# Convolution taps moved to later steps, and one subtraction put earlier, in a two-layer decoder step

## The reference, cut to what matters

```
h = rmsnorm(x);  z = h @ w_in          # one projection for all branches
y_a = mLSTM(q, k, v, gates)            # 4 heads of 128, decayed scores, matrix memory
u = glu_a * sigmoid(glu_b)
y_b = silu(layernorm(dwconv31(u)))     # depthwise, causal, 31 taps, 512 channels
y_c = sliding-window attention with sinks  # 8 query heads, 2 key heads, window 128
x += (g_a*y_a + g_b*y_b + g_c*y_c) @ w_out
x += (silu(dwconv3(h2 @ w_gate)) * (h2 @ w_up)) @ w_down
```

## Time and profile before

| | before |
|---|---|
| median of 3 runs | 1087.49 us |
| the profiled execution | 1089.15 us, span 1087.1 us |
| PE busy | 1028.8 us (95% of the span) |
| DVE busy | 782.5 us (72%) |
| ACT busy | 558.9 us (51%) |
| POOL busy | 38.3 us (4%) |
| mean granted clock of TensorE | 0.976 of full |

### The profile page before, as it was taken

One profiled execution on the slowest core, in us unless ns is written; L12 is line 12 of the kernel. 1 busy time (PEld: TensorE's weight loads), 2 busy tenths in 40 slices (PEclk: granted clock), 3 DMA queues, 4 the chain that ended last, 5 costly groups with the idle time before them and its releaser, 6 DMA issues.

```text
span 1087.1 us, 19523 instructions
## 1 busy us (share of the span) xinstructions
PE 1028.8 (95%) x7898; PEld 976.9 (90%) x7898; DVE 782.5 (72%) x1489; ACT 558.9 (51%) x1040; POOL 38.3 (4%) x55
## 2 busy tenths in 40 slices
PE   5999999899898999999979999998998989999997
PEld 3998889788898999999979998897888989999996
DVE  4577896656787778775565879874769877877563
ACT  3545555645534656553344456644654546665432
POOL 0010000003000000000000200000120000000000
PEclk9999999899999999999989999998999999999999
DMA  9654536355445676556576645462654657665561
GB/s 251 148 139 122 137 98 157 97 143 144 151 136 155 193 217 174 169 158 177 146 182 156 159 106 153 112 177 81 156 166 144 168 138 238 184 177 170 166 185 48
DMA packets 318643, 167.92 MB, mean 154 GB/s; under 512 B 25270, under 2 KB 317478, under 8 KB 318490
## 3 DMA queue, kind: packets, MB, share of 16 engines
q1 hardware_dynamic: 318410, 165.87, 56.0%
q10 hardware_dynamic: 144, 0.80, 0.2%
HBM read 160.11 MB, written 9.71 MB: 156 GB/s over the span
## 4 chain that ended last, share of the span: by engine, by line
PE 77%; DVE 9%; ACT 6%; DMA 4%; issue 3%; SPq 0%; DVEq 0%; ACTq 0%
PE ps_tile L883 16%; PE ps_tile L884 15%; PE ps_tile L885 15%; PE work L883 7%; PE work L885 7%; PE work L884 7%; ACT w_hi L1279 2%; DVE w_lo L1748 2%; DMA w_raw<-in_w_in 2%; DVE uc L1849 1%; DMA w_raw<-in_w_conv_out 1%; PE work L1117 1%; ACT scores L1413 1%; PE work L1119 1%; PE work L1127 1%
## 5 line engine op out<-in xcount | busy, mean ns | idle before, releaser
L1748 DVE TENSOR_TENSOR w_lo<-w_raw,w_hi 128x1024 fp32r<-128x1024 f32 (+1 forms) x288 | 341.4, 1192 | 135.0 <-ACT w_hi L1279 134.6
L1279 ACT ACTIVATE w_hi<-w_raw 128x1024 fp32r<-128x1024 f32 (+1 forms) x288 | 295.0, 1028 | 180.7 <-DMA w_raw<-in_w_in 78.3
L883 PE MATMUL ps_tile<-h_hi,w_hi 128*128 128x280 f32 (+2 forms) x944 | 284.7, 302 | 10.2 <-DVE h_lo L1758 10.2
L884 PE MATMUL ps_tile<-h_lo,w_hi 128*128 128x280 f32 (+2 forms) x944 | 277.0, 293 | 0.0
L885 PE MATMUL ps_tile<-h_hi,w_lo 128*128 128x280 f32 (+2 forms) x944 | 276.5, 293 | 0.0
L883 PEld LDWEIGHTS ps_tile<-h_hi,w_hi 128*128 128x128 f32 (+1 forms) x944 | 179.6, 190 | 16.9 <-issue 14.6
L884 PEld LDWEIGHTS ps_tile<-h_lo,w_hi 128*128 128x128 f32 (+1 forms) x944 | 179.4, 190 | 1.0
L885 PEld LDWEIGHTS ps_tile<-h_hi,w_lo 128*128 128x128 f32 (+1 forms) x944 | 179.0, 190 | 0.6
L883 PE MATMUL ps_tile<-xg_hi,w_hi 128*128 128x280 f32 (+1 forms) x368 | 107.7, 293 | 6.2 <-DVE x L1806 6.2
L1849 DVE SCALAR_TENSOR_TENSOR uc<-u_pad,vec,uc 128x272 f32<-128x272 f32 x240 | 108.4, 506 | 0.1
L885 PE MATMUL ps_tile<-xg_hi,w_lo 128*128 128x280 f32 (+1 forms) x368 | 107.2, 291 | 0.0
(11 more groups left out here) (348 smaller groups left out, 1836.7 us busy)
## 6 DMA issues: line engine op xcount, KB each, us to landing
w_raw<-in_w_in SPq DMA_DIRECT2D x98, 512.0 KB, 4.1
w_raw<-in_w_ffn_gate SPq DMA_DIRECT2D x44, 512.0 KB, 3.9
w_raw<-in_w_ffn_up SPq DMA_DIRECT2D x44, 512.0 KB, 3.9
w_raw<-in_w_ffn_down SPq DMA_DIRECT2D x32, 512.0 KB, 3.6
w_raw<-in_w_out SPq DMA_DIRECT2D x16, 512.0 KB, 3.6
w_raw<-in_w_ffn_down SPq DMA_DIRECT2D x14, 384.0 KB, 3.1
w_raw<-in_w_in SPq DMA_DIRECT2D x20, 256.0 KB, 3.6
c_head<-in_state_mlstm_c SPq DMA_DIRECT2D x8, 512.0 KB, 4.1
```

Source lines behind the costliest of these rows:

```text
L883: mm(out, hi[:, k, :], a_hi[:, k0 + k, f:T], start=first, stop=False, skip_group_check=True)
L884: mm(out, hi[:, k, :], a_lo[:, k0 + k, f:T], start=False, stop=False, skip_group_check=True)
L1279: go(h, r, ACT.Copy).then_inc(w_hi_ready, 1)
L1748: tt(lo, r, h.bitcast(F32), ALU.subtract).then_inc(w_split[n % SLOTS], 1)
```

## The change

`BUSY` gives other counts. In the attention steps 21 to 36 an odd step has 1 tap for 2, an even one 2 for 4. Steps 37, 38 and 42 have 5 for 4. Steps 43 to 50 have 7 for 4; these add up to more than 124, so that step 50 is left with 4. In a layer 24 taps leave steps 21 to 36, 3 go to steps 37 to 42 and 21 to steps 43 to 49.

On VectorE, `block_att_lo` moves ahead of `softmax_unit_2` within a step. Steps in which both stand are 29 (block 0, unit 3) and 33 (block 1, unit 5).

```diff
-BUSY = {10: 2, 14: 0, 15: 0, 16: 3, 17: 1, 18: 1, 19: 0, 20: 1, 39: 0, 40: 3, 41: 1, **{n: 2 for n in range(21, 37, 2)}}
+BUSY = {10: 2, 14: 0, 15: 0, 16: 3, 17: 1, 18: 1, 19: 0, 20: 1, 39: 0, 40: 3, 41: 1, 37: 5, 38: 5, 42: 5,
+        **{n: 1 if n % 2 else 2 for n in range(21, 37)}, **{n: 7 for n in range(43, 51)}}
 TAPS_AT = [BUSY.get(n, 4) if CONV_FROM <= n < CONV_TO else 0 for n in range(N_PIECES)]
...
                     if n == 20:
                         output_sample()
+                    if n - 1 in VALUES_AT[1::2]:
+                        block_att_lo(VALUES_AT.index(n - 1) // 2)
                     if n - 2 in SCORES_AT:
                         softmax_unit_2(SCORES_AT.index(n - 2))
                     if n == 22:
                         sample_att_lo()
-                    if n - 1 in VALUES_AT[1::2]:
-                        block_att_lo(VALUES_AT.index(n - 1) // 2)
```

## The result

The changed kernel takes 1093.14 us (median, 12 runs), the one before 1087.13, timed beside it: a ratio of 1.0056 (95% interval 1.0041 to 1.0071), or 6.0 us more (4.5 to 7.7). One of the twelve runs took 4555.12 us and is left out of the ratio; without it the median is 1092.92. A second measurement of the same pair (e8) gave 1.0058 (1.0039 to 1.0077). The forecast was +4.0 and 1091.5.

A forecast was written before the change was run, and what follows sets the result against it. TensorE was taken to set the pace, VectorE time counting only ahead of decay_d or att_lo products. Terms -3.3 + 1.9 + 0.5 + 4.9 gave +4.0 us, a median of 1091.5, range 1084 to 1097.

The forecast's parts named there:

- the second rival: VectorE bounds the attention steps, so both waits there go and mLSTM steps hide the taps: 1082, chance 0.08.
- the third: Rival: only step 43's taps cost, as TensorE comes later to step 48 anyway: -0.8, 1086.7, chance 0.17.
- a wait of about 2.4 in step 48: Sign that the forecast is right: TensorE waits about 2.4 us for decay_d in step 48 of both layers.
- The order, -3.3: Step 29's att_lo ahead of the softmax scaling shortens step 30: 2.2 us in layer 0, 1.06 in layer 1.
- The 1.2 for the low clock in layer 0: Part of the order's gain: step 30's 16 products take 1.86 us instead of 3.08 at full clock.
- Taps leaving the attention, 0: Steps 21 to 36 lose 24 taps a layer, 10 us of VectorE, with no gain in time.
- Step 43, +1.9: Three more taps ahead of head 0's decay_d: +1.24 us a layer, less 0.6 in all for low clock.
- Step 45, +0.5: Seven taps collide with GpSimd's gating product and end later: +0.25 us a layer, between 0 and 0.5.
- Steps 46 and 47, +4.9: Both tap blocks delay decay_d of head 2: +2.4 us in layer 0, +2.5 in layer 1.
- Steps 48 to 50, 0: decay_d of head 3 is 2.5 us later, but TensorE comes 2.4 later too: 0, at most 1.24.
- The first rival: The new wait in step 48 draws a low-clock stretch: +6.4 to +10 us, 1094 to 1097.5, chance 0.23.
- The sum: All terms for the whole kernel together: -3.3 + 1.9 + 0.5 + 4.9 = +4.0 us, median 1091.5.

The follow-up runs named there:

- e8: The changed kernel again, without edit, timed against the kernel before for a second profile: 1093.36 us, ratio 1.0058.
- e7: The control: the kernel before, without edit, timed against itself: 1087.01 us, ratio 0.9990.
- e3: The kernel before with 7 taps in step 43 for 4, leaving step 50 with 1: 1088.88 us, ratio 1.0010.
- e2: The kernel before with only the tap counts changed, the order as before: 1094.48 us, ratio 1.0065 to the kernel before.
- e5: The changed kernel with 4 taps in steps 43, 45, 46, 47, and 10 in 42, 12 in 44, 9 in 48, 8 in 49: 1095.77 us.
- e12: The changed kernel with step 43 empty and 11 taps in step 42: 1081.98 us, ratio 0.9966 to the kernel before.
- e6: The kernel before with the new order and step 43's four taps moved to step 42: 1076.65 us, ratio 0.9881.

## Why the prediction was right, and where it was not

- **The direction and the reason held.** The taps are free where they were, as the windows show, and are paid where they went. The two main paying places are those named, steps 44 and 48. With that the second rival is out (the attention steps did not get shorter by the taps that left), and so is the third (step 48 does wait). Of the signs named, one did not come: a wait of about 2.4 in step 48; it is 1.19 and 1.54.
- **The order, -3.3.** Measured alone -2.8 (-4.6 to -1.0). At equal clock it is 1.12 and 0.94, against the forecast's 1.0 and 1.06. The 1.2 for the low clock in layer 0 was taken from one execution; e7 shows an execution of the same kernel without it. It should have been a bound and not a full term.
- **Taps leaving the attention, 0.** Right in both orders.
- **Step 43, +1.9.** Step 44 grew by the 1.24 forecast, in both layers of the changed kernel and of e3; the part that falls into the low clock anyway showed in e3 as 0.5, the forecast's 0.6. It was luck of that execution: in layer 0 of the changed kernel the clock was full for the whole wait and 0.50 for 10 us behind it (211.4 to 221.4), and step 45 took 0.62 longer and not less (in layer 1 it took 0.53 less).
- **Step 45, +0.5.** It came as 0.36 and 0.48 in step 46: the collision with GpSimd came there as worked out (3.49 for seven taps, 2.97 without it).
- **Steps 46 and 47, +4.9.** This term was mis-sized in the profiled executions: step 48 grew by 1.44 and 1.23, not 2.4 and 2.5. In layer 0, VectorE's run grew by 1.94 and not 2.48, since the term priced the collision of the earlier trace rows as staying; and TensorE already came 2.04 later to step 48 (237.19 for 235.15) while VectorE's run began only 1.54 later, so 0.50 of the 1.94 had been paid before: 1.44 is left. In layer 1 the same working gives 1.97 less 0.74, 1.23. Where the collision did stay, layer 1 of e2 (3.39 for the seven taps), step 48 grew by 2.04.
- **Steps 48 to 50, 0.** Right: nothing in layer 0, and in layer 1 0.43 in step 50, where the control alone differs by 0.23 (7.05 for 6.82). e5 suggests why: there TensorE was not held up in step 48, and eight taps ahead of decay_d of head 3 cost 2.0 of waiting in layer 0; in the changed kernel the wait in step 48 had covered its seven. That it was this and not the eighth tap was not taken apart.
- **The first rival** holds in part. It was said to decide from a wait of about 2 us on; waits of 1.34 and 1.58 drew the low clock (e2 in layer 0, e12 in layer 1), one of 2.35 didn't (e2 in layer 1).
- **The sum.** The forecast's +4.0 lies between the traces' +2.5 and the medians' +6.0. Most of the chance stood on no measurable difference; the result, 0.56%, lies just above that bound. The two halves, timed apart, give +4.3, so the total is of the right size. That it came so near is in part luck: against the traces the term for steps 46 and 47 was 2.2 too high (4.9 for 2.67), and the 1.5 to 3 us named under e8, for which the sum has no term, make up for it.

What the prediction didn't see was the better move. It priced step 43 at 0.415 a tap, and e6's expectation took that price for the way back too. Adding three cost 1.24 a layer in step 44, since the low clock was there already; removing four gained 5.5 in layer 0 (4.6 against the control), since it went, and 2.9 in layer 1, where some of it stayed.

## What to carry to other kernels

Filler work belongs where its engine waits, not where its stage is least busy: look for what stands right behind it, and whether another engine is waiting for that. A wait of TensorE that has a low-clock stretch behind it is worth more than its length, so the first tap to move is the one ahead of such a wait, and to price it by the length of the tap alone is too little. When waits stand in series, the later one gets only what the earlier didn't already take.

## What the runs showed of the hardware that was not expected

GpSimd's product of 128 x 272 took 0.76 us beside four taps that lost 0.5; beside seven it took 3.13 while they lost nothing (238.62), and 0.94 while they lost 0.52 (225.87). In these three one of the two pays. The Trainium skill ("SBUF — State Buffer", Who interferes with whom) says that a VectorE instruction with two inputs in SBUF contends with a GpSimd one that reads SBUF, and that the order of issue decides who blocks; the trace agrees with the first half. The second is said there of single instructions; for whole blocks of taps it doesn't hold, as the taps had begun first in both of the changed kernel's cases, and lost in one of them.
